# Issuing the indexer products of the prompt in pairs, one row half of the array per PSUM bank

## The reference, cut to what matters

```python
rel = jax.nn.relu(jnp.einsum('nqhe,nke->nqhk', iqi, ik) * (IDX_HD ** -0.5))
score = jnp.einsum('nqhk,nqh->nqk', rel, iwi * (IDX_HEADS ** -0.5))
```

## Time and profile before

| | before |
|---|---|
| median of 3 runs | 2926.79 us |
| the profiled execution's own time | 2930.68 us |
| its span, first to last instruction | 2928.2 us |
| PE busy | 2746.4 us (94%) |
| DVE busy | 1486.4 us (51%) |
| ACT busy | 916.8 us (31%) |
| mean granted TensorE clock | 0.972 |

### The profile page before, as it was taken

How to read it: one execution, slowest core, us unless ns; L and a number is a source line. 1 busy time by engine, 2 the same in 40 slices (tenths; PEclk the granted TensorE clock), 3 DMA queues, 4 the chain that set the end, 5 groups by cost and what they waited for, 6 DMA issues and landing times. The chain is left out here.

```text
span 2928.2 us, 61465 instructions
## 1 busy us (share of the span) xinstructions
PE 2746.4 (94%) x25518; PEld 2533.6 (87%) x25518; DVE 1486.4 (51%) x2602; ACT 916.8 (31%) x1742; POOL 147.7 (5%) x301
## 2 busy tenths in 40 slices
PE   6999999999999988989989999999999999887998
PEld 6998988898787987889989899989878788787997
DVE  4333353236736586963343325432577268498433
ACT  3222342232222442232232224332333215323322
POOL 2100000000010000000001000100000200000001
PEclk8999999999999999989999999999999989998999
DMA  5323325632233222034333243265322422300543
GB/s 181 90 73 89 103 77 162 192 82 67 59 97 86 59 63 90 3 110 137 111 82 91 54 103 112 62 202 150 89 63 59 112 59 77 110 3 17 158 135 128
DMA packets 398475, 277.99 MB, mean 95 GB/s; under 512 B 34460, under 2 KB 368332, under 8 KB 394606
## 3 DMA queue, kind: packets, MB, share of 16 engines
q1 hardware_dynamic: 397278, 263.50, 32.5%
q10 hardware_dynamic: 912, 10.50, 0.9%
HBM read 237.75 MB, written 36.18 MB: 94 GB/s over the span
## 5 line engine op out<-in xcount | busy, mean ns | idle before, releaser
L326 PE MATMUL acc<-h_hi,in_w_hi 128*128 128x272 f32 x3968 | 888.1, 305 | 12.8 <-DVE in_w_lo L356 9.3
L326 PE MATMUL acc<-h_hi,in_w_lo 128*128 128x272 f32 x3968 | 824.2, 289 | 0.0
L326 PE MATMUL acc<-h_lo,in_w_hi 128*128 128x272 f32 x3968 | 822.7, 289 | 0.0
L326 PEld LDWEIGHTS acc<-h_hi,in_w_hi 128*128 128x128 f32 x3968 | 629.2, 190 | 97.5 <-issue 69.5
L326 PEld LDWEIGHTS acc<-h_lo,in_w_hi 128*128 128x128 f32 x3968 | 627.2, 190 | 0.0
L326 PEld LDWEIGHTS acc<-h_hi,in_w_lo 128*128 128x128 f32 x3968 | 624.2, 190 | 0.0
L356 DVE TENSOR_TENSOR in_w_lo<-in_w_raw,in_w_hi 128x512 fp32r<-128x512 f32 x496 | 345.9, 703 | 376.7 <-ACT in_w_hi L352 373.8
L352 ACT CAST in_w_hi<-in_w_raw 128x512 fp32r<-128x512 f32 x496 | 303.1, 617 | 367.8 <-PE acc L326 291.5
L326 PE MATMUL dr_bank<-over_both,out_weights 128*128 128x272 f32 x1984 | 280.2, 288 | 1.7 <-DVE over_both L713 1.7
L326 PEld LDWEIGHTS dr_bank<-over_both,out_weights 128*128 128x128 f32 x1984 | 260.7, 188 | 2.0 <-DVE over_both L713 2.0
L356 DVE TENSOR_TENSOR out_weights<-regions,out_weights 128x512 fp32r<-128x512 f32 x128 | 88.3, 692 | 184.1 <-ACT out_weights L352 184.0
(11 more groups left out here) (417 smaller groups left out, 3332.1 us busy)
## 6 DMA issues: line engine op xcount, KB each, us to landing
in_w_raw<-in_w_in SPq DMA_DIRECT2D x488, 256.0 KB, 2.9
region<-in_cache_sb_kv SPq DMA_DIRECT2D x128, 256.0 KB, 3.1
regions<-in_w_out SPq DMA_DIRECT2D x128, 256.0 KB, 2.8
regions<-in_cache_dsa SPq DMA_DIRECT2D x64, 160.0 KB, 2.2
region<-x_spill SPq DMA_DIRECT2D x32, 272.0 KB, 3.5
x_spill<-region SPq DMA_DIRECT2D x32, 272.0 KB, 2.1
mix_spill<-mix SPq DMA_DIRECT2D x6, 1088.0 KB, 5.4
mix_back<-mix_spill SPq DMA_DIRECT2D x6, 1088.0 KB, 7.4
```

The lines of the kernel that those rows point to most:

```text
L326: last = pe.matmul(self.place(i)[:, c, 0:HALF_N], w[:, u % RING, t, :], part[f][:, HALF_N * c:HALF_N * c + HALF_N], start=first and w is k ...
```

## The change: what it does

PE issues `index(q, h)` and `index(q, h + 1)` directly one after the other for even h. The even head (rows 0 to 63 of the array) writes bank 0, the odd head (rows 64 to 127) writes bank 3. Each product waits for the rectification of the product two before it, which was the last one in its bank, instead of the one just before. The stream units that followed each product are kept: the yields after the odd head stay where they were, so a pair is followed by 6 units in blocks 0 and 1 and by 4 after that. Bank 3 is also the bank of `apply`. So from block 2 on each product also waits for ACT's copies out of it (`kept`, all four heads of block q - 2), and `apply` of block q waits until all products of block q + 1 are rectified. ACT's rectification reads bank 0 or 3 by the head's parity. DVE, POOL and SP are unchanged.

```diff
         def index(q, h):
             u, w, r = 8 * q + h, P * (q + 1), h % 2
-            if u >= 1:
-                pe.wait_ge(self.rectified, u)
-            pe.matmul(bank[:, 0, 0:w], ft[64 * r:64 * r + 64, 7 + h // 2, P * q:P * q + P], ft[64 * r:64 * r + 64, 6, 0:w],
+            if u >= 2:
+                pe.wait_ge(self.rectified, u - 1)
+            if q >= 2:
+                pe.wait_ge(self.kept, 4 * (q - 1))
+            pe.matmul(bank[:, 3 * r, 0:w], ft[64 * r:64 * r + 64, 7 + h // 2, P * q:P * q + P], ft[64 * r:64 * r + 64, 6, 0:w],
                       start=True, stop=True).then_inc(self.multiplied, 1)
...
             v = 4 * q + h - 2
             if h >= 2:
                 pe.wait_ge(self.copied, v + 1)
+                pe.wait_ge(self.rectified, 8 * min(q + 2, QB))
...
         for h in range(8):
-            index(0, h)
+            if h % 2 == 0:
+                index(0, h)
+                index(0, h + 1)
             yield 3
         for q in range(1, QB + 1):
             for h in range(8 if q < QB else 0):
-                index(q, h)
+                if h % 2 == 0:
+                    index(q, h)
+                    index(q, h + 1)
                 yield 3 if q == 1 else 2
...
-            act.activation(self.rel[:, u % 2, 0:w], bank[:, 0, 0:w], ACT.Relu, scale=0.125).then_inc(self.rectified, 1)
+            act.activation(self.rel[:, u % 2, 0:w], bank[:, 3 * (h % 2), 0:w], ACT.Relu, scale=0.125).then_inc(self.rectified, 1)
```

## The result

The changed kernel takes 2894.33 us (median of four runs, 2893.75 to 2900.75) against 2927.79 for the kernel before in the same comparison (2926.07 to 2930.51). The ratio is 0.9884, with a 95% interval of 0.9868 to 0.9899: between 29.6 and 38.6 us less. Forecast were 2897.5 us and a gain of 29.3. The profiled execution is the slowest of the four, 2900.75 us with a span of 2898.9; its span is 29.3 us under the span before.

The account below looks back on a forecast made before the run. PE was taken to bound the index phases and DVE the attend phases; 32 saved insertions, 29.8 us, less 0.5 for pairing, give 29.3 off the median: 2926.8 - 29.3 = 2897.5 us, range 2891 to 2908.

Parts of the forecast that it names:

- What bounds: Sparse attention stage: PE's path sets the index phases, DVE sets the attend phases, which move forward without getting shorter.
- The wait removed was worth nothing: Before each index product: waiting for the rectification just before costs nothing; entry gaps are 0.33 to 0.34 us with or without.
- What a pair costs: Index products on PE: a pair costs one product plus 0.015 us, since the two row halves run side by side.
- The sum: Index phases: each pair saves one insertion, 14.9 us per layer, 29.8 in both, less 0.5: 29.3 us.
- one half-rate stretch more or less: After PE's long waits the granted clock falls to half; one such stretch moves the time 3.4 us at most, either way.
- The added waits: Waits for `kept` and for rectifications in `apply`: cost 0, upper ends 0.5, 1.4 and 2.9 us, 4.8 together.
- ACT's and DVE's longer chain behind a pair: Both rectifications free the banks 2.3 us after a 512-key pair starts; the next comes at 4.2, nearly 2 us to spare.
- Program order: Rival at the pairs: odd head's first pass starts only beside even head's second, three slots; gain 20.8, 2906.0 us; chance 0.07.
- No overlap: Rival at the pairs: the second product costs its two passes, only 0.40 us each saved; gain 12.8, 2914.0 us; chance 0.06.
- Absorbed: Rival in the index phases: DVE sets them too, so the time stays at 2926 us; chance 0.03.
- starved on ACT: Rival: PE stalls before pairs for both rectifications; slower from 0.92 us per pair, 2936 us at 1.2; chance 0.04.
- The price of two semaphore increments: One increment per product of a pair: 32 pairs would lose 1.0 us, gain 28.3; left out of the sum.

Follow-up runs that it names:

- the banks alone: The changed kernel with its waits and two banks, but each product back at its old place among the stream units: 2927.2 us, ratio 0.9993 to before.
- both profiles of the change: The changed kernel profiled twice, the second time with no edit: 2894.33 us, ratio 0.9884, then 2896.55 us, ratio 0.9892 to before.
- the pairs in one row half: The changed kernel with heads reordered so both products of a pair lie in the same row half: 2915.31 us, ratio 0.9949 to before.
- the wait covered: The changed kernel with 8 instead of 3 stream units ahead of PE's wait for the samples' normalized weights: 2884.15 us, ratio 0.9852 to before.

## Why the prediction was right, step by step

*What bounds.* That an index phase costs what PE costs, and an attend phase what DVE costs, held: the index phases shrank by 29.5 us and the attend phases, all together, kept their length within 0.8 us, where those of the kernel with the banks alone moved by 2.4. The one small gain that the range allowed there, a DVE chain that starts earlier, can't be told apart: the attend phases of blocks 2 and 3 together are 0.3 us shorter in the first layer and 0.8 in the second, in both profiles of the change, and with the banks alone 1.1 and 0.0.

*The wait removed was worth nothing:* shown by the banks alone, whose index phases are as long as before.

*What a pair costs.* One product plus 0.015 us was forecast from the retention's scores. The index line's four passes last 0.01 us longer than its two did at 512 keys, and the widths that no row of before had showed nothing new: the insertion is 0.62 us at 128 keys and 1.26 at 512, where 0.63 and about 1.27 were forecast. The 0.40 us that don't depend on width, and passes of 0.106 us per 128 columns, were confirmed from the other side by the pairs in one row half: 12.4 us in 32 pairs is 0.39 each. What the prediction named as their parts does not fill them, though: the entry gap has 0.09 us over a couple's 0.25 and the exit 0.11, together 0.20. The other 0.20 lies between the start of the product and the next couple, 0.41 us for two passes of 0.106.

*The sum:* 29.3 us forecast, 29.5 in the index phases of both profiles, and 33.5 by the medians of both timed comparisons (34.0 and 31.6 by their ratios). What lies between is not located in the timed runs. In the second profile, which has it, it lies in stages that the change doesn't touch, the delta rules of both layers above all, and for the first of them the clock is the likely reason. The forecast allowed 3.4 us for one half-rate stretch more or less; the two profiles of one kernel differ by about such a stretch, 3 us in the samples' stage.

*The added waits:* cost 0 was taken, with 4.8 us as the upper end. The pair of block 2 in the first layer starts at 694.23, with an entry gap of 0.34 us (the view ends ahead of the pair's last two passes):

```profile
693.59 0.27 ACT L1947 COPY mix<-bank 128x128 f32<-128x128 f32 x1 [0.71 <-PE bank L1827]
...
693.89 0.41 PE L326 MATMUL acc<-h_hi,in_w_lo 128*128 128x272 f32 x2
...
694.23 0.59 PE L1799 MATMUL bank<-regions 64*128 64x384 f32 x2
```

L1947's copy ended at 693.86, 0.37 us ahead, as reckoned. Nothing waited.

*ACT's and DVE's longer chain behind a pair* had been given 2 us to spare. In block 3 (timeline of ACT and DVE):

```profile
744.44 0.60 ACT L1920 ACTIVATE regions<-bank 128x512 f32<-128x512 f32 x1 [3.04 <-PE bank L1799]
...
745.72 0.61 ACT L1920 ACTIVATE regions<-bank 128x512 f32<-128x512 f32 x1
...
746.62 0.75 DVE L1996 SCALAR_TENSOR_TENSOR region<-regions,region 128x512 f32<-128x512 f32 x1
```

The products are done 1.1 us after the pair's start at 743.28, as reckoned. The second rectification does not follow the first at once: a tile copy and a weight cast come between, and it ends at 746.33, 3.05 us after the start and not 2.3. The next pair starts at 747.55 by the trace, so the slack is 1.2 us, not 2. This is the first pair of block 3 and the tightest of all 32; at the other pairs of that block the second rectification ends 2.25 us after the start, and 2.0 us are left, as reckoned. It did not decide, but by an estimate from these rows two or three more casts of 0.6 us in that gap would have used it up.

*The rivals.* Program order is out: three pass slots would have given 1.68 us per insertion at 512 keys, and 1.26 were measured. In the trace's records the four matmuls of the pair of block 3 start at 743.280, 743.287, 743.814 and 743.820, and the increments are on the last two: the odd head's first pass runs beside the even head's first. The rule in the Trainium skill ("TensorE: Matmul & The Clock Gate", What overlaps and what doesn't), that matmuls start and end strictly in program order, does not hold for these if PE's queue has both passes of the even head ahead of the odd head's, as the prediction took it. Whether it has them so, or already in turns, the trace doesn't show. No overlap (2.1 us) is what the pairs in one row half show. Absorbed and starved on ACT are out by the index phases' length and by PE's list of waits. The price of two semaphore increments, about 31 ns for each pair by an estimate from the figures of the Trainium skill ("TensorE: Matmul & The Clock Gate", The cost: per-tile semaphore tail), is not seen on PE either: from the index line to the next couple it is 0.42 us with two increments and 0.41 with one.

## What to carry to other kernels

If small matmuls interrupt a stream of full-array matmuls, price the interruption from the stream's own rhythm: here 0.40 us of 0.61 to 1.26 was entering and leaving, whatever the size. Issue 64-row products in pairs that use both row halves, each half with its own bank as here; the second is then all but free, while a pair in the same half only shares entry and exit. A gain of a few microseconds at one place may not show in the whole time when the granted clock elsewhere is lower, so look at the stretches behind PE's long waits before calling a gain lost.

## What I had not expected of the hardware

The same 34 us of the program round a 3.7 us wait ran at a mean granted clock of 0.65 in one execution of the change and 0.75 in another, worth about 3 us; with the wait covered it was 0.85. And the two passes of an f32 product need not stay together on the array: both halves' passes take turns, so that four passes in two row halves take the time of two (1.13 us against 1.12), where four in one half take 1.98.
